# One written order for the mixing stage of block 1, in place of evenly spaced merging

## The chip, the cores and the metric

The kernel runs on one core of one Trainium2 chip. The metric is the device time of one execution in microseconds (us), the median of several. The core has five engines with queues of their own that run in order and meet only at semaphores: TensorE (PE, matrix products), VectorE (DVE), ScalarE (ACT), GpSimd (POOL) and SyncE (SP, which here issues the weight loads).

## The reference

The program is two layers of a first block (block 1: mixing, then an MLP) followed by two layers of another block (block 2), on 512 tokens of width 1024. The change concerns the mixing of block 1, which runs twice:

```python
h = rms_norm(x, g_mix_pre)
u = h @ w_in                       # 1024 -> 3200
aq, ak, av, cu, rq, rk, rv, rg = jnp.split(u, SPLITS, axis=-1)
y_att = chunk_attention(aq, ak, av, rel_bias)      # 6 heads, softmax with a bias table
y_conv = conv_module(cu, conv_w, conv_b, ...)      # gate, 31 depthwise taps, layer norm, silu
y_ret = retention(rq, rk, rv, rg)                  # 6 heads, rotary, decay mask, layer norm, gate
mix = jnp.concatenate([y_att, y_conv, y_ret], axis=-1) @ w_out
x = x + rms_norm(mix, g_mix_post)
```

## The kernel before

**Tiles.** Activations lie transposed, features on the 128 partitions and all 512 tokens along the row. The projection `w_in` is cut into units of 128 output features. For each unit ACT copies the raw weights to a rounded high part (L945), DVE takes the low part (L1406), and PE makes 24 matmuls (8 tiles of 128 inputs, three products each, L2027 to L2029, called one projection below). A unit's split runs two units ahead: it is issued by ACT and DVE at the place of an earlier projection in the order of steps.

**Names in the order.** `q`, `k`, `v` with a number 0 to 2 are the attention projections of a pair of heads, `cg` and `ca` those of the convolution, `rq`, `rk`, `rv`, `rg` those of retention; a name with `f` at its end is the projection, and the same name without it the transposition by PE that follows (L2242). `sq`, `sk` are the rotary swaps: one matmul (L2247), then three DVE operations (L1625, L1626, L1628). `rs0` to `rs23` are retention scores of one head and one block of 128 keys, with n = 512, 384, 256 or 128 columns (L2280; head h and block j are number 4h + j); DVE multiplies each by the decay mask while it empties the bank (L1715). `r_pv` is the product with the values (L2306), `r_out` ACT's copy of it. `lm`, `cm` are means (L2291, L2284) and `lv`, `cv` variances (L2294, L2288) of the layer norms. `taps` k is tap k of the convolution, two DVE operations (L1608), 62 in all.

**Banks.** Projections, transpositions, swaps, scores `rs`, means and variances take two PSUM banks (0 and 1) in turn, in the order in which they stand. PE may write the next of them only when the one before last has been emptied, by ACT for some and by DVE for others.

**Attention.** There are twelve attention steps (three pairs of heads, four blocks of queries). A step j goes through: scores on PE (L2107, L2109); bias and maximum on DVE (L1540, L1542); exponentials on ACT (L1029); reciprocal on DVE (L1528); scaling on POOL (L883); transpositions on PE (L2118); a copy on DVE for even steps (L1521) or ACT for odd (L1035); the product with the values on PE (L2129); after each fourth step ACT's copy of the result (L1039).

**What sets the order.** A list of steps is made once, and each engine walks it and issues its own part of each step. Before, an entry `att` k carries for PE the scores of step k, the transpositions of step k-2 and the value product of step k-3; for ACT the exponentials of k-1, the copy of k-2 and the output of k-3; for DVE the copy of k-2. An entry `weigh` k carries for DVE the reciprocal of k-1 and the bias and maximum of k. These entries, the projections, the retention heads and the taps are merged by `weave` (L234), which places each list at even distances within each of six stretches (L310 to L321):

```python
steps += weave(in_order(ret_qkv(1), "rv1"), heads(0), attend(8, 11), taps(16, 23))
```

Of the kernel before, what the change touches and what calls it, by code (L numbers as in the profile page):

```python
# [19 lines left out]
ALU = mybir.AluOpType  # L20
# [3 lines left out]
P = 128  # L24
D = 1024
S = 512
# [10 lines left out]
HD = 64  # L37
# [48 lines left out]
ACT_STEPS, DVE_STEPS = (2, 18), (79, 37)  # L86
NSA_PAIRS, T_LAG, O_LAG, P_BUFS = 3, 4, 5, 4
# [153 lines left out]

def plan_block1():
# [57 lines left out]
    def attend(a, z):  # L300
        return [(what, k) for k in range(a, z) for what in ("att", "weigh") if what == "att" or k <= n_att]

    def taps(a, z):
        return [("taps", k, k + 1) for k in range(a, z)]

# [3 lines left out]
    steps = qkv(0)  # L309
    steps.append(query(1))  # L310
    steps += [add(f"cg{t}", "fm", 1408 + 128 * t, frees="act", dst=A_SG + S * t, func="Sigmoid", keep=t == 0) for t in range(2)]
    steps.append(("g", "v0"))
    steps += [add(f"ca{t}", "fm", 1152 + 128 * t, frees="dve", glu=t) for t in range(2)]
# [6 lines left out]
    steps += weave([("mix", 0), gate(0), ("mix", 1), ("g", "lm0"), ("g", "cm"), gate(1), ("mix", 2), ("g", "lv0"), ("c_square",), gate(2), ("g", "cv"), ("g", "lm1"), ("early", 0), ("g", "lv1")], heads(2))  # L320
    steps += [("ahead",), ("early", 1), ("g", "lm2"), ("gated",), ("r_square", 2), ("rmul", 0), ("rmul", 1), ("early", 2)]  # L321
    steps += [("conv_out",), ("mix", 3), ("mix", 4), ("ln_set",), ("g", "lv2"), ("mix", 5), ("mix", 6), ("rmul", 2), ("mix", 7)]
# [145 lines left out]
def build(nc, x_in, cst, msk, tab1, tab2, scratch, out, w):  # L468
    with ExitStack() as ctx:
# [465 lines left out]
        def _(act):  # L935
# [85 lines left out]
            def attend(c, l, j):  # L1021

                e = j - EXP_LAG
                if 0 <= e < n1:
                    st, n = stat[:, e % 4, :], att_e[e]["n"]
                    act.wait_ge(c.maxed.sem, c.maxed.at(l, e + 1))
                    for head in HEADS:
                        p_ = att_p(e, head, n)
                        act.activation(p_, p_, ACT.Exp, bias=st[:, head:head + 1], accum_out=st[:, 2 + head:3 + head]).then_inc(c.exped.sem, 1)  # L1029
                k = j - TURN_LAG  # L1030
                if 0 <= k < n1 and k % 2:
                    act.wait_ge(c.turned.sem, c.turned.at(l, k + 1))
                    if k >= 2:
                        act.wait_ge(c.pv.sem, c.pv.at(l, k - 1))
                    act.activation(att_pt(k), bank[:, 4:6, 0:att_e[k]["n"]], ACT.Copy).then_inc(c.pt[1].sem, 1)  # L1035
                k = j - PV_LAG
                if 0 <= k < n1 and att_e[k]["i"] == QT - 1:
                    act.wait_ge(c.pv.sem, c.pv.at(l, k + 1))
                    act.activation(g(MIX + S * att_e[k]["p"]), bank[:, 6, :], ACT.Copy).then_inc(c.o_done.sem, 1)  # L1039
# [150 lines left out]
            for l in range(LAYERS):  # L1190
# [7 lines left out]
                for s in b["steps"][4:]:  # L1198
                    if s[0] == "g":
                        group(c, b, l, b["groups"][s[1]])  # L1200
                    elif s[0] == "att":
                        attend(c, l, s[1])
# [198 lines left out]
        def _(dve):  # L1401
# [112 lines left out]
            def attend(c, l, j):  # L1514

                k = j - TURN_LAG
                if 0 <= k < n1 and k % 2 == 0:
                    dve.wait_ge(c.turned.sem, c.turned.at(l, k + 1))
                    if k >= 2:
                        dve.wait_ge(c.pv.sem, c.pv.at(l, k - 1))  # L1520
                    dve.tensor_copy(att_pt(k), bank[:, 4:6, 0:att_e[k]["n"]]).then_inc(c.pt[0].sem, 1)  # L1521

            def weigh(c, l, j):

                k = j - EXP_LAG
                if k >= 0:
                    dve.wait_ge(c.exped.sem, c.exped.at(l, 2 * k + 2))
                    dve.reciprocal(stat[:, k % 4, 4:6], stat[:, k % 4, 2:4]).then_inc(c.rcp.sem, 1)  # L1528
                if j < n1:
                    e, n, st = att_e[j], att_e[j]["n"], stat[:, j % 4, :]  # L1530
                    dve.wait_ge(c.qk.sem, c.qk.at(l, j + 1))
                    if e["i"] == 0:
                        dve.wait_ge(c.h_in[e["p"] % 2].sem, c.h_in[e["p"] % 2].at(l, e["p"] // 2 + 1))
                    if j >= 2:
                        dve.wait_ge(c.turned.sem, c.turned.at(l, j - 1))
                    if j >= 4:
                        dve.wait_ge(c.scaled.sem, c.scaled.at(l, 2 * j - 6))
                    p_ = pair_tile(A_P[j % 2], n)
                    table = g(A_H[e["p"] % 2], 2 * S).rearrange("p (e n) -> p e n", e=2)[:, :, n - 1::-1]
                    dve.tensor_tensor(p_, bank[:, 2:4, 0:n], table, ALU.add).then_inc(c.biased.sem, 1)  # L1540
                    dve.wait_ge(c.biased.sem, c.biased.at(l, j + 1))
                    dve.tensor_reduce(st[:, 0:2], p_, AXX, ALU.max, negate=True).then_inc(c.maxed.sem, 1)  # L1542
# [277 lines left out]
            for l in range(LAYERS):  # L1820
# [7 lines left out]
                for s in b["steps"][4:]:  # L1828
                    if s[0] == "g":
                        group(c, b, l, b["groups"][s[1]])  # L1830
                    elif s[0] == "att":
                        attend(c, l, s[1])
                    elif s[0] == "weigh":
                        weigh(c, l, s[1])
# [189 lines left out]
        def _(pe):  # L2024
# [71 lines left out]
            def attend(c, b, l, j):  # L2096

                if j < n1:
                    p, i, n = att_e[j]["p"], att_e[j]["i"], att_e[j]["n"]
                    q = P * i  # L2100
                    if i == 0:
                        need(c, b, l, f"q{p}", f"k{p}", f"v{p}")
                    if j:
                        pe.wait_ge(c.biased.sem, c.biased.at(l, j))
                    for head in HEADS:
                        r = half(head)
                        pe.matmul(bank[:, 2 + head, 0:n], g(A_Q + S * p + q, P, r), g(A_K + S * p, n, r), start=True, stop=False)  # L2107
                    for head in HEADS:
                        ins = pe.matmul(bank[:, 2 + head, q:q + P], identb, chunked, start=False, stop=True)  # L2109
                    ins.then_inc(c.qk.sem, 1)  # L2110
                k = j - TURN_LAG
                if 0 <= k < n1:
                    if k:
                        pe.wait_ge(c.pt[(k - 1) % 2].sem, c.pt[(k - 1) % 2].at(l, (k - 1) // 2 + 1))
# [6 lines left out]
                if 0 <= k < n1:  # L2121
                    p, i = att_e[k]["p"], att_e[k]["i"]
                    pe.wait_ge(c.pt[k % 2].sem, c.pt[k % 2].at(l, k // 2 + 1))
                    if i == 0 and p:
                        pe.wait_ge(c.o_done.sem, c.o_done.at(l, p))
# [518 lines left out]
```

## Time and profile before

| | us |
|---|---|
| median of 3 runs | 3427.54 |
| lowest and highest | 3426.94, 3428.37 |
| the profiled execution: its time | 3425.86 |
| the profiled execution: its span, first to last instruction | 3424.0 |
| of the span: PE busy | 3349.4 |
| DVE, ACT, POOL busy | 1670.1, 1223.3, 236.9 |

The mixing of block 1 lies at 54 to 255 us of the span in the first layer and some 640 us later again in the second. A row of the time line gives start, duration, engine, line, operation and tile; in brackets stands how long the engine was idle before it and who ended that. A PE row of one float32 matmul counts as x2. Matmuls overlap in part, so a duration is longer than the distance to the next start; distances between starts are what adds up to time.

### The profile page before, as it was taken

To read this page: it belongs to the slowest core of one execution; us is meant where nothing else is said; L and a number is where in the kernel's file an instruction comes from. 1 tells how busy PE (TensorE), PEld (TensorE's weight loads), DVE (VectorE), ACT (ScalarE), POOL (GpSimd) and SP (SyncE) were. 2 spreads that over 40 slices of the span, in tenths; PEclk is the share of its full clock that TensorE was granted. 3 is DMA by queue.
4 is the path that set the end of the run, shared out by engine and by line. 5 is a ranking of instruction groups with operands and counts; after the bars stand their busy time and mean duration, and the time that the engine had idled before them with its cause. 6 is when DMAs were issued, how large, how long until landed. Compare 5 with 4: busy or idle time off the path is not lost.

```text
span 3424.0 us, 42157 instructions
## 1 busy us (share of the span) xinstructions
PE 3349.4 (98%) x15716; PEld 2623.2 (77%) x15716; DVE 1670.1 (49%) x2158; ACT 1223.3 (36%) x1831; POOL 236.9 (7%) x268
## 2 busy tenths in 40 slices
PE   8999999999999999999999999999999999999999
PEld 6657888776688887888766688888888876678887
DVE  6755443566544335443646554435443554654444
ACT  4343122432522233232454433334223454542333
POOL 1200000011010000000102300002000101300000
PEclk9999999999999999999999999999999999999999
DMA  6213322321243232332321133333333321023332
GB/s 170 64 47 87 96 95 98 92 81 50 68 101 97 98 104 74 96 95 97 87 60 29 31 104 93 97 98 94 98 98 98 93 72 34 19 88 98 93 97 74
DMA packets 434263, 288.19 MB, mean 84 GB/s; under 512 B 44529, under 2 KB 412317, under 8 KB 433897
## 3 DMA queue, kind: packets, MB, share of 16 engines
q1 hardware_dynamic: 431272, 280.02, 28.2%
q0 software_dynamic: 2736, 4.58, 0.9%
q10 hardware_dynamic: 144, 2.10, 0.2%
q8 instruction: 72, 1.18, 0.1%
q14 instruction: 39, 0.31, 0.0%
HBM read 284.53 MB, written 2.13 MB: 84 GB/s over the span
## 4 chain that ended last, share of the span: by engine, by line
PE 93%; DVE 3%; ACT 2%; issue 1%; DMA 0%; SPq 0%; DVEq 0%; ACTq 0%
PE bank L2027 27%; PE bank L2028 27%; PE bank L2029 27%; PE bank L2157 1%; PE bank L2203 1%; PE bank L2063 1%; PE bank L2179 1%; PE bank L2280 1%; PE bank L2247 1%; PE bank L2107 1%; ACT whi L945 1%; PE bank L2564 0%; DVE G L1562 0%; PE bank L2051 0%; PE bank L2129 0%
## 5 line engine op out<-in xcount | busy, mean ns | idle before, releaser
L2027 PE MATMUL bank<-hh,whi 128*128 128x512 f32 x2768 | 1093.1, 395 | 9.5 <-DVE G L1715 3.5
L2029 PE MATMUL bank<-hh,wlo 128*128 128x512 f32 x2768 | 1079.8, 390 | 0.0
L2028 PE MATMUL bank<-hl,whi 128*128 128x512 f32 x2768 | 1079.8, 390 | 0.0
L1406 DVE TENSOR_TENSOR wlo<-raw,whi 128x1024 fp32r<-128x1024 f32 (+2 forms) x534 | 647.0, 1213 | 318.1 <-ACT whi L945 303.7
L945 ACT ACTIVATE whi<-raw 128x1024 fp32r<-128x1024 f32 (+2 forms) x534 | 546.4, 1034 | 265.7 <-PE bank L2029 264.9
L2027 PEld LDWEIGHTS bank<-hh,whi 128*128 128x128 f32 x2768 | 521.3, 188 | 141.7 <-issue 33.1
L2029 PEld LDWEIGHTS bank<-hh,wlo 128*128 128x128 f32 x2768 | 521.0, 188 | 109.7
L2028 PEld LDWEIGHTS bank<-hl,whi 128*128 128x128 f32 x2768 | 521.4, 188 | 108.1 <-issue 2.6
L2027 PE MATMUL bank<-fshi,whi 128*128 128x512 f32 (+1 forms) x1358 | 525.9, 387 | 3.0 <-ACT G L1090 1.6
L2028 PE MATMUL bank<-fslo,whi 128*128 128x512 f32 (+1 forms) x1358 | 522.0, 384 | 0.0
L2029 PE MATMUL bank<-fshi,wlo 128*128 128x512 f32 (+1 forms) x1358 | 521.9, 384 | 0.0
L1755 DVE TENSOR_TENSOR fslo<-G,fshi 128x512 fp32r<-128x512 f32 x152 | 104.7, 692 | 460.8 <-ACT fshi L1130 460.8
L2027 PEld LDWEIGHTS bank<-fshi,whi 128*128 128x128 f32 x1358 | 255.6, 188 | 60.6 <-issue 5.6
L2029 PEld LDWEIGHTS bank<-fshi,wlo 128*128 128x128 f32 x1358 | 256.1, 189 | 51.0
L2028 PEld LDWEIGHTS bank<-fslo,whi 128*128 128x128 f32 x1358 | 255.9, 188 | 50.5 <-issue 1.0
L1130 ACT ACTIVATE fshi<-G 128x512 fp32r (+1 forms) x152 | 95.3, 631 | 539.8 <-PE bank L2029 539.8
L1286 ACT ACTIVATE G<-G 128x512 f32<-128x512 f32 x88 | 55.6, 632 | 619.2 <-DVE G L1907 619.1
L1907 DVE TENSOR_TENSOR G<-bank,G 128x512 f32<-128x512 f32 x88 | 60.9, 692 | 243.9 <-PE bank L2029 229.9
L1090 ACT ACTIVATE G<-bank 128x512 f32<-128x512 f32 x66 | 39.4, 597 | 279.7 <-PE bank L2029 279.7
L1910 DVE TENSOR_TENSOR G<-bank,G 128x512 f32 (+1 forms) x88 | 60.9, 692 | 147.4 <-PE bank L2029 147.4
L850 POOL TENSOR_TENSOR G<-G 128x512 f32<-128x512 f32 x21 | 33.3, 1585 | 1423.0 <-ACT G L971 1420.1
L1870 DVE TENSOR_TENSOR G<-bank,G 128x512 f32<-128x512 f32 x64 | 44.3, 692 | 167.0 <-PE bank L2029 158.9
(257 smaller groups left out, 2562.8 us busy)
## 6 DMA issues: line engine op xcount, KB each, us to landing
raw<-in_ffn_w_gate SPq DMA_DIRECT2D x88, 512.0 KB, 3.8
raw<-in_ffn_w_up SPq DMA_DIRECT2D x88, 512.0 KB, 3.8
raw<-in_ffn_w_down SPq DMA_DIRECT2D x88, 512.0 KB, 3.5
raw<-in_w_in SPq DMA_DIRECT2D x78, 512.0 KB, 4.0
raw<-in_w_up SPq DMA_DIRECT2D x64, 512.0 KB, 4.0
raw<-in_w_down SPq DMA_DIRECT2D x64, 512.0 KB, 3.4
raw<-in_w_out SPq DMA_DIRECT2D x16, 512.0 KB, 3.9
raw<-in_w_in SPq DMA_DIRECT2D x18, 256.0 KB, 3.5
```

What stands on the lines that cost most here:

```text
L945: act.activation(slot3(whi, s, m), slot3(raw, s, m), ACT.Copy).then_inc(c.hi_done.sem, 1)
L1090: act.activation(g(gr["dst"], S, r), bk[r[0]:r[1], :], act_func(gr.get("func")), scale=gr.get("scale", 1.0)).then_inc(evac, 1)
L1130: act.activation(fshi[:, 2 if paired else t % 2, :], f_tile(t + more), ACT.Copy).then_inc(c.f_hi.sem, 1)
L1286: act.activation(rt[t], tmp[t], ACT.Silu).then_inc(c.silu.sem, 1)
L1406: dve.tensor_tensor(slot3(wlo, s, m), slot3(raw, s, m), slot3(whi, s, m).bitcast(F32), ALU.subtract).then_inc(c.lo_done.sem, 1)
L1755: dve.tensor_tensor(fslo[:, fs, :], f_tile(t + more), fshi[:, fs, :].bitcast(F32), ALU.subtract).then_inc(c.f_lo.sem, 1)
L1870: dve.tensor_tensor(tmp[j % 2], bank[:, OUT_BANK + 1 + j, :], rstd, ALU.mult).then_inc(c.up_norm.sem, 1)
L1907: dve.tensor_tensor(tmp[t], bank[:, 4 + j, :], rstd, ALU.mult).then_inc(c.g_norm.sem, 1)
L1910: dve.tensor_tensor(f, bank[:, 4 + j, :], rstd, ALU.mult).then_inc(c.u_norm.sem, 1)
L2027: pe.matmul(o, wh, ah, start=start, stop=False)
L2028: pe.matmul(o, wh, al, start=False, stop=False)
L2029: return pe.matmul(o, wl, ah, start=False, stop=stop)
```

## The change

The attention entries are taken apart. There are now entries for PE alone (`a_scores`, `a_turns`, `a_values`), for ACT alone (`a_exps`, `a_move_act`, `a_out`) and for DVE alone (`a_bias`, `a_rcp`, `a_move_dve`), each in the same order within its engine as before. The six stretches are gone: one string of 216 letters says from which of six lists the next step is taken (f: projections and what follows them, p, a, d: attention on PE, ACT, DVE, h: retention heads, t: taps). Every instruction is issued as often as before, with the same operands and the same semaphores to wait on; the lags between the parts of an attention step are free. The change acts in both layers of block 1. The first six projections, the end of the stage (from `lv1` on) and block 2 keep their order.

```diff
+MIXING1_ORDER = (
+    "dffpftftdpatdtftadapdfpdfadpttpfdfpddtptpafdfppttttfadadpddafptdtpptffpapafpapddhfttadhppfpddhhhahtdhpftpafhpdahthppfdtp"
+    "hhfhadtdfpaatphdpdhfphdahphdhffttahhthfphtphftttffhhhphahffffhhhfhfffhhhhfhhhffffffffffffffffffff")
...
+def merged(order, **lists):
+
+    queues = {letter: iter(steps) for letter, steps in lists.items()}
+    return [next(queues[letter]) for letter in order]
...
-    steps += weave(in_order(qkv(1), "v1"), attend(0, 3), taps(0, 5))
-    r0 = ret_qkv(0)
-    steps += weave(in_order(r0, "rv0"), attend(3, 6), taps(5, 11))
-    steps += weave(in_order(qkv(2), "v2"), attend(6, 8), taps(11, 16))
-    steps += weave(in_order(ret_qkv(1), "rv1"), heads(0), attend(8, 11), taps(16, 23))
-    steps += weave(in_order(ret_qkv(2), "rv2"), heads(1), attend(11, n_att + PV_LAG), taps(23, TAPS))
...
+    for j in range(n_att + PV_LAG):
+        by_pe += staged(j, "a_scores") + staged(j - TURN_LAG, "a_turns") + staged(j - PV_LAG, "a_values")
+        by_act += staged(j - EXP_LAG, "a_exps") + staged(j - TURN_LAG, "a_move_act", odd) + staged(j - PV_LAG, "a_out", last)
+        by_dve += staged(j - TURN_LAG, "a_move_dve", even) + staged(j - EXP_LAG, "a_rcp") + staged(j, "a_bias")
...
+    steps = first_six + merged(MIXING1_ORDER, f=prepared, p=by_pe, a=by_act, d=by_dve, h=heads(0) + heads(1) + heads(2), t=[("taps", k, k + 1) for k in range(TAPS)])
```

The three pieces below show how it moves instructions. Line numbers are those of each version; the changed one is some 15 lines longer, so that L1406 of before is L1423 of the change, L2280 is L2298 and so on.

**First piece, DVE, from the gate of the convolution on.** TENSOR_TENSOR `wlo` is the low part of a weight unit, L1729 empties a `ca` bank, COPY from `bank` empties `k1`, and a TENSOR_TENSOR of `bank,G` with 128x2x128 columns and the TENSOR_REDUCE behind it are the bias and maximum of attention step 0. Before:

```order
L1728 MEMSET G 128x30
L1729 TENSOR_TENSOR G<-bank,G 128x512
L1406 TENSOR_TENSOR wlo<-raw,whi 128x1024
L1728 MEMSET G 128x30
L1729 TENSOR_TENSOR G<-bank,G 128x512
L1605 TENSOR_SCALAR G<-G,prm 128x512 x2
L1406 TENSOR_TENSOR wlo<-raw,whi 128x1024
L1738 COPY G<-bank 128x512
L1540 TENSOR_TENSOR G<-bank,G 128x2x128
L1542 TENSOR_REDUCE stat<-G 128x2
```

And now:

```order
L1555 TENSOR_TENSOR G<-bank,G 128x2x128
L1557 TENSOR_REDUCE stat<-G 128x2
L1423 TENSOR_TENSOR wlo<-raw,whi 128x1024
L1743 MEMSET G 128x30
L1744 TENSOR_TENSOR G<-bank,G 128x512
L1423 TENSOR_TENSOR wlo<-raw,whi 128x1024
L1743 MEMSET G 128x30
L1744 TENSOR_TENSOR G<-bank,G 128x512
L1620 TENSOR_SCALAR G<-G,prm 128x512 x2
L1423 TENSOR_TENSOR wlo<-raw,whi 128x1024
```

The bias of step 0 stood behind both gates, two weight parts, tap 0 and the copy of `k1`; it now stands ahead of all of them.

**Second piece, PE, at the projection `rk1`.** L2107 and L2109 are attention scores of step 8, L2118 transpositions of step 6, L2129 the value product of step 5, L2280 (L2298) the retention scores. Before:

```order
L2029 MATMUL bank<-hh,wlo 128x512
L2107 MATMUL bank<-G 128x128 x2
L2109 MATMUL bank<-m_sb 128x128 x2
L2118 MATMUL bank<-c_sb,G 128x128 x6
L2129 MATMUL bank<-G 64x128 x4
L2280 MATMUL bank<-G 128x512
L2280 MATMUL bank<-G 128x384
L2027 MATMUL bank<-hh,whi 128x512
```

And now:

```order
L2046 MATMUL bank<-hh,wlo 128x512
L2298 MATMUL bank<-G 128x512
L2123 MATMUL bank<-G 128x128 x2
L2125 MATMUL bank<-m_sb 128x128 x2
L2135 MATMUL bank<-c_sb,G 128x128 x6
L2044 MATMUL bank<-hh,whi 128x512
```

`rs4` (512 columns) stood directly ahead of `rs1` and `rk1`; it now stands ahead of the attention work, and `rs1` (384) has gone behind `rk1`, next to `rs5`.

**Third piece, ACT, around the projection `q2`.** L1090 (L1103) empties a projection's bank, L1094 (L1107) that of a transposition, L1029 (L1040) are exponentials, L945 (L958) the high part of a weight unit, L1035 (L1047) the copy of step 3. Before:

```order
L1029 ACTIVATE G,stat<-G,stat 128x128 x2
L1035 ACTIVATE G<-bank 128x1024
L1094 ACTIVATE G<-bank 128x4x128
L945 ACTIVATE whi<-raw 128x1024
L1090 ACTIVATE G<-bank 128x512
L1029 ACTIVATE G,stat<-G,stat 128x256 x2
```

And now:

```order
L1107 ACTIVATE G<-bank 128x4x128
L1040 ACTIVATE G,stat<-G,stat 128x128 x2
L1047 ACTIVATE G<-bank 128x1024
L1040 ACTIVATE G,stat<-G,stat 128x256 x2
L958 ACTIVATE whi<-raw 128x1024
L1103 ACTIVATE G<-bank 128x512
```

The exponentials of step 5 (256 columns) stood behind the weight part and the emptying of `q2`; they now stand ahead of both.

## Rows read from the trace of the kernel before

**Rows 1.** The page, part 1: busy time of each engine

```profile
PE 3349.4 (98%) x15716; PEld 2623.2 (77%) x15716; DVE 1670.1 (49%) x2158; ACT 1223.3 (36%) x1831; POOL 236.9 (7%) x268
```

**Rows 2.** Windows: stretch, length, busy us (instructions) by engine, granted clock, DMA share, GB/s

```profile
54.05:233.90 179.85, 174.47 (x860) 118.27 (x860) 118.54 (x182) 59.35 (x112) 27.74 (x26) 1.00 0.22 62
```

**Rows 3.** Waits of PE, 50 to 260 us: us in total, times, longest

```profile
PE bank L2027 <- DVE G L1715: 1.8, 2, 0.9
...
PE bank L2280 <- ACT G L1090: 0.5, 2, 0.3
```

**Rows 4.** The same in the second layer, 640 to 860 us

```profile
PE bank L2107 <- DVE G L1540: 1.1, 1, 1.1
```

**Rows 5.** Time line of PE, 65 to 81 us

```profile
72.49 0.70 PE L2107 MATMUL bank<-G 64*128 64x256 f32 x4 [1.11 <-DVE G L1540]
```

**Rows 6.** Time line of PE, 127 to 139 us

```profile
136.50 1.12 PE L2280 MATMUL bank<-G 64*128 64x512 f32 x4
138.50 0.47 PE L2027 MATMUL bank<-hh,whi 128*128 128x512 f32 x1 [0.88 <-DVE G L1715]
```

**Rows 7.** Time line of PE, 156 to 164 us

```profile
156.69 0.48 PE L2280 MATMUL bank<-G 64*128 64x128 f32 x2
...
157.87 1.13 PE L2247 MATMUL bank<-G,c_sb 128*128 128x512 f32 x2
158.92 0.92 PE L2107 MATMUL bank<-G 64*128 64x384 f32 x4
159.77 0.28 PE L2109 MATMUL bank<-m_sb 128*128 128x128 bf16 x2
...
160.21 1.09 PE L2129 MATMUL bank<-G 128*64 128x128 f32 x16
161.14 0.82 PE L2306 MATMUL bank<-G 128*64 128x256 f32 x8
161.89 0.66 PE L2242 MATMUL bank<-c_sb,G 128*128 128x128 f32 x4
163.28 1.09 PE L2280 MATMUL bank<-G 64*128 64x512 f32 x2 [0.73 <-issue]
```

**Rows 8.** Time line of PE, 182 to 187 us

```profile
183.88 0.70 PE L2280 MATMUL bank<-G 64*128 64x256 f32 x2
184.81 0.70 PE L2280 MATMUL bank<-G 64*128 64x256 f32 x2 [0.24 <-DVE G L1628]
185.44 0.87 PE L2306 MATMUL bank<-G 128*64 128x384 f32 x4
```

**Rows 9.** Time line of PE, 204.5 to 208 us

```profile
204.80 1.67 PE L2280 MATMUL bank<-G 64*128 64x512 f32 x4
206.71 1.12 PE L2291 MATMUL bank<-G,c_sb 128*128 128x512 f32 x2 [0.24 <-DVE G L1715]
```

**Rows 10.** Time line of PE, 217 to 222 us

```profile
217.24 1.45 PE L2280 MATMUL bank<-G 64*128 64x256 f32 x4
219.13 1.10 PE L2294 MATMUL bank<-G,c_sb 128*128 128x512 f32 x2 [0.43 <-ACT G L1070]
```

**Rows 11.** Groups of DVE by form, 54.05 to 233.9 us: busy us, mean ns | idle before

```profile
L1406 DVE TENSOR_TENSOR wlo<-raw,whi 128x1024 fp32r<-128x1024 f32 x20 | 24.4, 1220 | 12.3 <-ACT whi L945 12.3
```

**Rows 12.** Time line of POOL, with and without taps beside it

```profile
100.33 3.43 POOL L883 TENSOR_SCALAR G<-G,stat 128x512 f32<-128x512 f32 x2 [6.96 <-DVE stat L1528]
...
141.45 3.11 POOL L883 TENSOR_SCALAR G<-G,stat 128x512 f32<-128x512 f32 x2 [11.57 <-DVE stat L1528]
```

**Rows 13.** Time line of DVE, at 101 us

```profile
100.92 1.40 DVE L1608 SCALAR_TENSOR_TENSOR G<-G,prm 128x512 f32<-128x512 f32 x2
```

**Rows 14.** The chain that ended last, 181 to 186 us: start, us, what

```profile
184.07 0.70 DVE G L1628
```

**Rows 15.** Windows as in rows 2, after the stage's end, in both layers

```profile
240.00:250.00 10.00, 7.57 (x24) 5.24 (x23) 5.41 (x9) 8.38 (x12) 0.00 (x0) 0.83 0.37 101
...
880.00:890.00 10.00, 7.57 (x31) 5.38 (x30) 5.47 (x9) 7.97 (x12) 0.00 (x0) 1.00 0.32 90
```

More of the change, by code:

```diff
@@ L320, in plan_block1, with staged @@
-    steps += weave([("mix", 0), gate(0), ("mix", 1), ("g", "lm0"), ("g", "cm"), gate(1), ("mix", 2), ("g", "lv0"), ("c_square",), gate(2), ("g", "cv"), ("g", "lm1"), ("early", 0), ("g", "lv1")], heads(2))
-    steps += [("ahead",), ("early", 1), ("g", "lm2"), ("gated",), ("r_square", 2), ("rmul", 0), ("rmul", 1), ("early", 2)]
-    steps += [("conv_out",), ("mix", 3), ("mix", 4), ("ln_set",), ("g", "lv2"), ("mix", 5), ("mix", 6), ("rmul", 2), ("mix", 7)]
+    def staged(k, what, wanted=range(n_att)):
+        return [(what, k)] if 0 <= k < n_att and k in wanted else []
@@ new lines, in plan_block1 @@
+    first_six = qkv(0)
+    first_six.append(query(1))
+    first_six += [add(f"cg{t}", "fm", 1408 + 128 * t, frees="act", dst=A_SG + S * t, func="Sigmoid", keep=t == 0) for t in range(2)]
+    prepared = [("g", "v0")]
+    prepared += [add(f"ca{t}", "fm", 1152 + 128 * t, frees="dve", glu=t) for t in range(2)]
+    prepared += in_order(qkv(1), "v1")
+    prepared += in_order(ret_qkv(0), "rv0")
+    prepared += in_order(qkv(2), "v2")
+    prepared += in_order(ret_qkv(1), "rv1")
+    prepared += in_order(ret_qkv(2), "rv2")
@@ new lines, in plan_block1 @@
+    prepared += [("mix", 0), gate(0), ("mix", 1), ("g", "lm0"), ("g", "cm"), gate(1), ("mix", 2), ("g", "lv0"), ("c_square",), gate(2), ("g", "cv"), ("g", "lm1"), ("early", 0), ("g", "lv1")]
+    prepared += [("ahead",), ("early", 1), ("g", "lm2"), ("gated",), ("r_square", 2), ("rmul", 0), ("rmul", 1), ("early", 2)]
+    prepared += [("conv_out",), ("mix", 3), ("mix", 4), ("ln_set",), ("g", "lv2"), ("mix", 5), ("mix", 6), ("rmul", 2), ("mix", 7)]
+    steps = first_six + merged(MIXING1_ORDER, f=prepared, p=by_pe, a=by_act, d=by_dve, h=heads(0) + heads(1) + heads(2), t=[("taps", k, k + 1) for k in range(TAPS)])
@@ new lines, in att_turns @@
+            def att_turns(c, l, k):
+                if k:
+                    pe.wait_ge(c.pt[(k - 1) % 2].sem, c.pt[(k - 1) % 2].at(l, (k - 1) // 2 + 1))
+                pe.wait_ge(c.scaled.sem, c.scaled.at(l, 2 * k + 2))
+                for head in HEADS:
+                    for kt in range(att_e[k]["i"] + 1):
+                        ins = pe.transpose(bank[:, 4 + head, P * kt:P * kt + P], att_p(k, head, att_e[k]["n"])[:, P * kt:P * kt + P], ident)
+                ins.then_inc(c.turned.sem, 1)
@@ L2105, in attend, with att_values @@
+            def att_values(c, l, k):
+                p, i = att_e[k]["p"], att_e[k]["i"]
+                pe.wait_ge(c.pt[k % 2].sem, c.pt[k % 2].at(l, k // 2 + 1))
+                if i == 0 and p:
+                    pe.wait_ge(c.o_done.sem, c.o_done.at(l, p))
+                for kt in range(i + 1):
                     for head in HEADS:
                         r = half(head)
-                        pe.matmul(bank[:, 2 + head, 0:n], g(A_Q + S * p + q, P, r), g(A_K + S * p, n, r), start=True, stop=False)
@@ L2120, in attend @@
-                k = j - PV_LAG
[L2121 to L2125, printed above, removed]
-                    for kt in range(i + 1):
-                        for head in HEADS:
-                            r = half(head)
-                            ins = pe.matmul(bank[r[0]:r[1], 6, P * i:P * i + P], g(A_V + 384 * kt + HD * (2 * p + head), HD),
-                                            att_pt(k)[:, head, P * kt:P * kt + P], start=kt == 0, stop=kt == i)
-                    ins.then_inc(c.pv.sem, 1)
+                        ins = pe.matmul(bank[r[0]:r[1], 6, P * i:P * i + P], g(A_V + 384 * kt + HD * (2 * p + head), HD),
+                                        att_pt(k)[:, head, P * kt:P * kt + P], start=kt == 0, stop=kt == i)
```

152 lines of the change are left out of this document (71 added, 81 removed).

## The prediction

> **What bounds the kernel now.** I read the busy times first: PE is busy for 98% of the span, DVE for half and POOL hardly at all [rows 1]. So time goes down only where PE stands still, or where its own work gets shorter, and the change issues the same matmuls. The windows then say how much stands still in the stretch that is re-ordered: from 54.05 to 233.90 us PE is busy 174.47 of 179.85 us [rows 2], 5.4 us idle. A wait costs more than its idle time, because matmuls that follow each other overlap and the first ones behind a wait don't; I therefore take distances between starts. The waits by releaser show what PE waited for there: DVE's emptying of a score bank (L1715), ACT's emptying of a projection (L1090) and others [rows 3]. The second layer shows the same pattern; its wait for the bias at L1540 is 1.1 us [rows 4], that of the first 1.11 [rows 5]. I count one layer and double it. DVE has 118.54 and ACT 59.35 us of work in 179.85 us [rows 2]: neither is short of time on the whole, the waits come from where a step stands in a queue, and that is what the change touches.
>
> **The waits that the new order takes away,** each as the distance to PE's next start less the time of the work itself.
> (a) Scores of step 1 wait 1.11 us [rows 5] for the bias of step 0, which stood on DVE behind the copy of `k1`. Now it stands ahead, and two projections (`ca1`, `k1`) lie on PE between the scores of step 0 and of step 1. Gain 1.1.
> (b) `rs4` with `rs1`, then `rk1`, takes 138.50 - 136.50 = 2.0 us, where the two scores pass in 1.1 [rows 6]; `rk1` waits for DVE to empty the bank of `rs4`. The row [rows 3] counts two such waits, the other before `rk2` (behind `rs12`, `rs9`). Now scores and transpositions lie between `rs4` and `rk1`, and for `rk2` the transpositions stand behind it and the value product and `rs12` ahead, so that its bank, that of `rs8`, is emptied during `rs12`. Gain 2 x 0.9 = 1.8.
> (c) `rs3` and `rs7` take 157.87 - 156.69 = 1.18 us for some 0.45 us of work, since the second bank is still that of a projection that ACT empties [rows 7]; `rs11` and `rs15` likewise, the second of two such waits [rows 3]. Now `rpv1` and the value product of step 6 stand between `rv1f` and `rs3`, and `sk2` with the transpositions of step 11 between `rs11` and `rs15`. Gain 2 x 0.73 = 1.5.
> (d) `rv1`, then `rs8`: 163.28 - 161.89 = 1.39 us for 0.6 [rows 7]: `rs8` needs ACT's copy of the transposition just made. Now `rq2` and a whole attention step stand between. Gain 0.8.
> (e) `rs10` and `rs14`: 185.44 - 183.88 = 1.56 us [rows 8], where one pass takes 0.63; `rs14` waits for DVE to finish the swap `sq2`. Now `rv2f`, 5.5 us, stands between. Gain 0.9.
> (f) `rs20` with `rs17`, then `lm0`: 206.71 - 204.80 = 1.91 us [rows 9] for 1.1. Gain 0.8.
> (g) `rs18` with `rs22`, then `lv0`: 219.13 - 217.24 = 1.89 us [rows 10] for 0.63; they waited for ACT to empty `rg1`, and `lv0` for a square that stood behind that too. Now `rs21` and `rpv8` stand between `rg1` and `rs18`. Gain 1.3.
> Sum 8.2 us.
>
> **What it gives back.** Two scores of a pair of heads that stand next to each other pass in the time of one: `rs4` with `rs1`, four instructions, shows 1.12 us [rows 6], `rs8` alone, two instructions, 1.09 [rows 7]. So what counts is the number of passes. Before there are 6 of 512 columns, 3 of 384, 3 of 256 and 4 of 128 (counting a pair by its longer half, and pairs parted by a wait alone as one, since I took their whole wait as gain). Now there are 5, 4, 5 and 4. With 1.1 us for 512 [rows 6], 0.85 for 384 (the distance at the attention scores of that width, 159.77 - 158.92, [rows 7]) and 0.63 for 256 [rows 8] that is -1.1 + 0.85 + 1.26 = 1.0 us more. And one new wait is sure: `rs16`, `rs20`, `rs17` now stand in one row, and the third needs the bank of the first emptied by DVE, the situation of (b): 0.9 us. The wait before `cv` stays, behind other scores. Together 1.9.
>
> **What moves and is hidden.** DVE gets the bias of step 0 ahead of a weight part and a `ca` bank. Behind it wait PE's `k1` (the weight part) and `ca1`'s successor in the bank. The scores of step 0 come behind one projection, at some 60 us; bias and maximum of 256 columns take under 1 us by their width against the 1024 columns of a weight part, which takes 1.2 us [rows 11]: ready at some 62 us, needed at 65.8, a projection later. ACT gets the exponentials of step 2 ahead of the copy of `v1`, and those of step 5 ahead of a weight part and of `q2`'s bank; the second is the longest wait that the change adds, and I work it out below as the rival that ends on the other side. The last operations (from `lv1` on) hang on PE's `lm1`, `lv1` and on the ACT and DVE work behind them, in unchanged order, so they move as a whole. SP's weight loads follow DVE's low parts, which are at most 6 us later in place and are used two units later; PE never waits for one of them in this stretch.
>
> **The sum.** 8.2 - 1.9 = 6.3 us per layer, 12.6 for both. On the profiled execution's own 3425.86 us that makes 3413.3. The median of the three runs is 1.7 us above that execution, so on the median's scale the forecast is 3427.54 - 12.6 = 3414.9 us.
>
> **A rule of the notes against the trace.** POOL's scaling of a step of 512 columns takes 3.11 us alone and 3.43 with two taps beside it [rows 12]; the two taps, 1.40 us for both [rows 13], began while POOL was at work and took no longer than elsewhere. So here the two engines hardly disturb each other: 0.3 us, on POOL. The Trainium skill, page "SBUF — State Buffer", section "Who interferes with whom", states that a VectorE instruction with two SBUF inputs and a GpSimd instruction that reads SBUF exclude each other, the later one waiting for the whole of the earlier. By that rule the taps would have waited; the trace does not bear it out at this place.
> As a mechanism of this kernel the question matters, and it is the first rival. Before, DVE's reciprocal is followed by the next step's bias, which reads PSUM, so POOL's scaling runs beside that. Now in 5 of 12 steps taps or a weight part follow the reciprocal (steps 0, 2, 3, 5, 9).
>
> **The rivals.**
> *DVE and POOL take turns.* If each tap waited for POOL's scaling, DVE would be 3.1 us later behind step 3 [rows 12]. The bias of step 4 is by my count ready 1.4 us before PE needs it, so PE would lose 1.7 us per layer: 3414.9 + 3.4 = 3418.3. For it only the 0.3 us of rows 12; against it the taps of rows 13. 10%.
> *The tight places give way.* Behind `sk1` PE has a value product and two retention products, 161.89 - 160.21 = 1.7 us [rows 7], and the transposition of `rv1`, 0.6, before `rq2` needs the bank; DVE needs three operations of 0.7 us for the swap [rows 14], 2.0 us since they overlap a little. That leaves 0.3 us. Behind `sk0` it is some 0.7 us before `q2`, at the transpositions of step 4 (behind four taps, reciprocal and POOL) 1.6. If all three come 1.3 us later than my count, PE loses 1.0 + 0.6 + some of the third and its restarts, about 2.5 us per layer: 3420. For it: my counts come from one walk along the queues, to 0.3 us at best. 14%, half of it within the bound of no change.
> *More is won.* `rs17`'s wait may be hidden, or the swaps' order save restarts: up to 1.5 us per layer, 3411.9. 12%.
> *The clock.* Behind the stage's end, PE's granted clock was 0.83 of full over 10 us in the first layer and 1.00 in the second, at the same work [rows 15]: a short spell at the lower of the two levels (1.2 GHz), worth 0.17 x 10 = 1.7 us, came after thinly filled PE time in one and not in the other. With all later work moved by 6 and 13 us such spells can fall otherwise, by one or two in either direction: 3411.5 to 3418.3. 8%.
> *ACT stands still and takes PE with it.* The exponentials of step 5 wait for its maximum, which on DVE stands behind four taps, and behind them on ACT wait the high part for `v2f` and `q2`'s bank, which `v2f` takes over. From the swap `sk0`'s end DVE needs 8 x 0.7 for the taps [rows 13], then 1.4 for bias and maximum (twice the 0.7 of an operation of that width, [rows 14]); ACT some 2.4 for exponentials, weight part and copy (an estimate: it is no slower than DVE at like widths), DVE 1.2 for the low part [rows 11]: 10.6 us, against `q2`, `k2` and an attention step on PE, 14 us. Margin 3.5 to 4 us. It costs time only beyond that, and makes the kernel slower only if DVE is more than 3.7 + 6.3 = 10 us late there, in each layer. At 13 us late it would be 3414.9 + 2 x 9.3 = 3433.5. Nothing in rows 13 shows taps of nearly three times their length. 3%.
>
> **How the numbers follow.** The forecast has 53%, with its own range 3412 to 3417.5. The range 3410 to 3421 takes in the larger gain, the turns of DVE and POOL, the clock and most of the tight places, and leaves out some 12%. A difference of 0.2% (6.9 us) is about what a measurement can tell from no change. Faster by more: 53 + 10 + 12 + 8 + half of 14, less some for what I have not seen, 0.85. Within: 0.11. Slower: 0.04.
>
> **What would show it.** In the changed kernel's time line PE's idle time from the first `ca` projection to `lv1` should fall from 5.4 us to near 2; the wait for L1540 should be gone, that for L1715 stand once, before `rs17`; `lv1` should begin some 6 us earlier in the first layer and 12 in the second; the waits behind it should be as before. The forecast is wrong if PE waits for L1628 before `q2` or `rq2`, for ACT before `v2f`, or for POOL before transpositions, and if taps beside L883 are longer than 0.75 us each.

## The result and the profile after

The changed kernel takes 3407.15 us (median of 5 runs, 3406.06 to 3410.7); the kernel before took 3427.54 us (median of its 5 runs beside it). The ratio is 0.9942, 95% interval 0.9928 to 0.9957: faster by 20.4 us. The prediction was 3414.9 us with a range of 3410 to 3421: the sign was right, the gain was larger than the range allowed. The changed kernel was run once more later (`after_again`): 3409.01 against 3426.01 us, ratio 0.9951 (0.9937 to 0.9964). The two measurements give 20.4 and 17.0 us.

The changed kernel's page, part 1 (engine, busy us, share, instructions), against [rows 1]:

```profile
PE 3337.7 (98%) x15712; PEld 2623.6 (77%) x15716; DVE 1672.0 (49%) x2158; ACT 1222.6 (36%) x1831; POOL 248.9 (7%) x268
```

PE is busy 11.7 us less with the same matmuls (four records are missing). So not only waits went: busy steps also follow each other at shorter distances. POOL is busy 12 us longer. The window of the re-ordered stretch, from the first `ca` projection to `lv1`, columns as in [rows 2]:

```profile
56.11:226.38 170.27, 168.92 (x859) 118.24 (x860) 119.79 (x182) 59.11 (x112) 33.00 (x26) 1.00 0.24 66
```

It is 170.27 us long where it was 179.85 [rows 2]: 9.6 us less per layer. PE's idle time fell from 5.4 to 1.35 us, which is 4.0 of it; the other 5.5 us are shorter distances between busy matmuls. The waits of PE between 50 and 250 us (engine, line, waited for: us in all, times, longest) that lie in this window, against [rows 3]:

```profile
PE bank L2298 <- DVE G L1730: 0.8, 1, 0.8
...
PE bank L2306 <- DVE G L1730: 0.4, 1, 0.4
```

The wait for the bias is gone, and the wait for DVE's emptying of a score bank stands twice, before `rs17` and before `cv`. The sum had both; the prediction's list of signs counted only the first. Where [rows 5] shows a wait of 1.11 us, the changed kernel's time line shows none:

```profile
73.37 0.70 PE L2123 MATMUL bank<-G 64*128 64x256 f32 x4
```

Below, a step's *distance* is the time from PE's start of it to PE's start of the next step, the measure that the prediction used. Between two executions of one kernel it repeats to 0.04 us or better, while their whole times scatter by several us. *The stretch* is the time from `v0` to `lv1`, 181.18 us before and 171.60 after.

**Where the 18.7 us between the two profiled executions are.** For an execution I add up: the start of `v0`, twice the stretch, and half of the time during which the trace shows the granted clock at the lower level (1.2 GHz), since work there takes twice as long. Here, with no time at the lower clock inside the stretch, what is left of the span is the same in both:

| | start of v0 | stretch | lower clock | rest of the span |
|---|---|---|---|---|
| before | 52.72 | 181.18 | 39.3 | 2989.3 |
| after | 54.79 | 171.60 | 36.0 | 2989.3 |

So -18.7 = +2.1 (a later start of the stretch in this execution, not an effect of the order, which is the same up to there) - 2 x 9.58 - 1.6 (clock). The rest agrees better than the account deserves: over the other runs without a lowered clock in the stretch it lies between 2987.7 and 2990.0 us. The clock's 1.6 us is one spell, at 244 us of the span, that of [rows 15]; it is gone, and the others lie at the same work as before. Nothing else behind `lv1` took part.

### The profile page after: what moved, and what is told of

Same layout as the page of the kernel before. It is cut to its first block, busy times and chain, and to the rows that moved or that the text cites. A ratio compares the mean times of both kernels' runs of the same rounds, so it can differ in the third digit from the quotient of the medians.

```text
span 3405.3 us, 42157 instructions
## 1 busy us (share of the span) xinstructions
PE 3337.7 (98%) x15712; PEld 2623.6 (77%) x15716; DVE 1672.0 (49%) x2158; ACT 1222.6 (36%) x1831; POOL 248.9 (7%) x268
## 3 DMA queue, kind: packets, MB, share of 16 engines
q8 instruction: 72, 1.18, 0.1%
## 4 chain that ended last, share of the span: by engine, by line
PE 93%; DVE 3%; ACT 2%; issue 1%; DMA 0%; SPq 0%; DVEq 0%; ACTq 0%
PE bank L2044 27%; PE bank L2046 27%; PE bank L2045 27%; PE bank L2175 1%; PE bank L2221 1%; PE bank L2080 1%; PE bank L2197 1%; PE bank L2298 1%; ACT whi L958 1%; PE bank L2265 1%; PE bank L2586 0%; PE bank L2123 0%; DVE G L1577 0%; PE bank L2147 0%; PE bank L2068 0%
## 5 line engine op out<-in xcount | busy, mean ns | idle before, releaser
L1423 DVE TENSOR_TENSOR wlo<-raw,whi 128x1024 fp32r<-128x1024 f32 (+2 forms) x534 | 646.9, 1213 | 309.8 <-ACT whi L958 295.5
L958 ACT ACTIVATE whi<-raw 128x1024 fp32r<-128x1024 f32 (+2 forms) x534 | 546.4, 1034 | 272.9 <-PE bank L2046 272.4
L1103 ACT ACTIVATE G<-bank 128x512 f32<-128x512 f32 x66 | 39.3, 596 | 249.5 <-PE bank L2046 249.4
```

Of the source, the lines that this page charges most:

```text
L958: act.activation(slot3(whi, s, m), slot3(raw, s, m), ACT.Copy).then_inc(c.hi_done.sem, 1)
L1103: act.activation(g(gr["dst"], S, r), bk[r[0]:r[1], :], act_func(gr.get("func")), scale=gr.get("scale", 1.0)).then_inc(evac, 1)
L1423: dve.tensor_tensor(slot3(wlo, s, m), slot3(raw, s, m), slot3(whi, s, m).bitcast(F32), ALU.subtract).then_inc(c.lo_done.sem, 1)
```

## Experiments

The experiments that start from the kernel before are written in the new form, with steps in one order; the diffs show the order, one step a line where it matters. S, T and V with a number are attention scores, transpositions and value product of that step; R is DVE's reciprocal, B its bias, t a tap.

### Does PE's order alone bring it, or that of ACT and DVE?

`pe_new`: PE's steps in the new order, ACT's and DVE's attention steps and the taps at their old places. `pe_old`: the reverse.

> PE's steps in the changed kernel's order; the attention steps and taps of ACT and DVE stay where they were before, each behind the same projection. Theory 1 (the gain is PE's order: fewer waits there and cheaper neighbours): only the wait for the bias of step 0 comes back, 1.3 us per layer, so the gain is 20.4 - 2.6 = 17.8 us: 3409.7 us. Rival (ACT's and DVE's places carry the gain): under half of it, 3417 us or more, with PE waits for biases or copies.

> The other half: PE's steps in the old order, the attention steps and taps of ACT and DVE at the changed kernel's places. Theory 1: only the wait for the bias of step 0 goes, 1.3 us per layer: 3427.5 - 2.6 = 3424.9 us. Rival (ACT's and DVE's places carry the gain): 3417 us or less.

Measured: 3444.72 us, ratio 1.0046 (1.003 to 1.0063), and 3445.6 us, ratio 1.0048 (1.0031 to 1.0065). Theory 1 fell in both, and so did the rival, which needed `pe_old` at 3417 us or less: either half alone is 18 us *slower* than the kernel before, with a stretch of 188.6 and 190.9 us. In `pe_new`, ACT's time line shows where the longest wait comes from:

```profile
124.64 0.60 ACT L1052 ACTIVATE G<-bank 128x512 f32<-128x512 f32 x1 [12.48 <-PE bank L2147]
125.14 1.99 ACT L958 ACTIVATE whi<-raw 128x1024 fp32r<-128x1024 f32 x2
```

and PE's, behind it:

```profile
129.03 1.22 PE L2123 MATMUL bank<-G 64*128 64x512 f32 x2 [4.43 <-DVE G L1555]
```

V3 has moved behind `v2f` on PE, but ACT's copy of its result (L1052) stands at its old place, ahead of two weight parts. ACT stands for 12.48 us, DVE's low parts and bias follow late, and the scores of step 7 wait 4.43 us. In `pe_old` the mirror image: DVE takes up the bias of step 0 ahead of the banks of `ca0` and `ca1`, while PE makes these scores only behind `ca1`. DVE waits 11.21 us, and `k1` 2.8 us for its bank:

```profile
67.19 0.43 DVE L1555 TENSOR_TENSOR G<-bank,G 128x256 f32<-128x256 f32 x1 [11.21 <-PE bank L2125]
```

The waits are not the whole loss. Behind the wait of 4.43 us PE's granted clock (the last number but two) was at its lower level:

```profile
129.00:132.40 3.40, 3.38 (x12) 1.88 (x13) 3.40 (x5) 1.31 (x4) 1.04 (x2) 0.50 0.47 138
```

The scores of step 7 take 2.20 us there, to the next step's start, for 1.18 in the changed kernel. In the two stretches of `pe_new` 30.7 us ran at the lower clock, in those of `pe_old` 17.1, in those of the kernel before and of the changed one none. Half of that, 15 and 9 us, is my estimate of the clock's part; against the kernel before the two stretches are 16.0 and 17.8 us longer in sum.

What follows: the gain belongs to no engine's order. A step that moves on one engine takes its releaser's and its reader's places with it.

### Do shorter distances come from the neighbour?

Of 9.58 us, 2.4 lie in steps that no term of my sum touched; the largest part is 1.2 us of attention transpositions. In the changed kernel five of them are no longer followed by a value product. Two runs put this neighbour back and take it away.

`glued`, from the changed kernel (and likewise V1, V2, V3, V5 behind T2, T3, T4, T6):

```diff
 T1
+V0
 rk0
 ...
 sq0
-V0
```

> The changed kernel with the value products 0, 1, 2, 3 and 5 put back directly behind the transpositions of steps 1, 2, 3, 4 and 6. Theory 1 (a step's time depends on the shape of its neighbour: a full-array transposition before a 64-column product costs 0.17 to 0.20 us more than before a projection): the distances of these transpositions go back from 0.36, 0.58, 0.79, 0.15, 0.58 to 0.54, 0.76, 0.99, 0.32, 0.76 us, 0.88 per layer in sum, 3407.2 + 1.8 = 3409.0 us. Rival (these were small waits that the changed ACT and DVE places removed): the distances stay, 3407.2 us.

`apart`, from the kernel before, the reverse:

> The kernel before, with these five value products parted from the transpositions as in the changed kernel, and nothing else moved (but for ACT's copy of step 3's values, which follows its product). Theory 1: the five distances fall as above, 0.88 us per layer: 3427.5 - 1.8 = 3425.7 us. Rival: the distances stay, and nothing is gained, 3427.5 us.

Measured: 3411.61 us, ratio 0.9961 (0.9946 to 0.9975), and 3426.2 us, ratio 0.9993 (0.9983 to 1.0002). Neither total can tell 1.8 us from the clock's scatter; the distances decide. In us, with the step that follows:

| | T1 | T2 | T3 | T4 | T6 |
|---|---|---|---|---|---|
| before (V follows) | 0.54 | 0.76 | 0.99 | 0.32 | 0.76 |
| after (a projection follows) | 0.36 | 0.58 | 0.79 | 0.15 | 0.58 |
| glued (V follows) | 0.54 | 0.76 | 0.97 | 0.32 | 0.76 |
| apart | 0.36 | 0.58 | 0.90 (rv0) | 0.15 | 0.76 (rs4) |
| values_full (full-array V follows) | 0.45 | 0.66 | 0.88 | 0.22 | 0.66 |

The distances follow the neighbour each way, 0.88 us per layer in `glued` and 0.62 in `apart`. Where another step than a projection came behind the transpositions in `apart`, which my expectation overlooked, the gain is less: half before `rv0` (transpositions), nothing before `rs4` (a score). The stretch is 0.79 us shorter in `apart`, and 1.50 us longer in `glued`: there `rk1` also stands directly ahead of `rs1` and `rs5`, which take 0.76 and 0.84 us for 0.43 and 0.58. The trace names no wait there; that `rs5` can't pass beside `rs1` because ACT has not yet emptied `rk1`'s bank fits it, but is not tested. PE's time line at T1, before and after:

```profile
87.28 0.61 PE L2118 MATMUL bank<-c_sb,G 128*128 128x128 f32 x4
87.81 0.44 PE L2129 MATMUL bank<-G 128*64 128x128 f32 x4
```

```profile
88.14 0.61 PE L2135 MATMUL bank<-c_sb,G 128*128 128x128 f32 x4
88.50 0.47 PE L2044 MATMUL bank<-hh,whi 128*128 128x512 f32 x1
```

The busy time of the transpositions is 0.61 in both; only the start of what follows tells the difference. `glued` and `apart` don't say why a value product starts later. It uses half of the array (`128*64`). `values_full` keeps the old order and gives it all of it:

```diff
-pe.matmul(bank[r[0]:r[1], 6, P * i:P * i + P], g(A_V + 384 * kt + HD * (2 * p + head), HD), ... start=kt == 0, stop=kt == i)
+pe.matmul(bank[:, 6, P * i:P * i + P], g(A_V + 384 * kt + HD * 2 * p, 2 * HD), ... start=kt + head == 0, stop=kt == i and head == 1)
```

> The kernel before, where a value product takes 128 columns of weights (both heads' values) in place of 64 for each head: all of TensorE's array in place of a half, so the shape is that of the transposition ahead of it. The two heads' results are summed into each other, so this part of the output is another. Theory 1 (what costs 0.17 to 0.20 us is the change of shape): the transpositions of steps 1 to 4 and 6 take 0.36, 0.58, 0.79, 0.15, 0.58 us though a value product still stands behind them, and so do those of the other steps; the products themselves take nearly twice as long, since two heads no longer pass side by side (0.12 us for each 128 columns by the 0.48 of a 512-column pass of the means: 14.4 against 8.4 us per layer). Time 3427.5 + 2 x (6.0 - 1.9) = 3435.7 us. Rival (the product's own wait or its start costs it): the distances stay at 0.54, 0.76, 0.99, 0.32, 0.76, and 3439.5 us.

Measured, one run: 3429.17 us. All eleven transpositions ahead of a value product are shorter, but by 0.09 us and not by 0.18:

```profile
88.40 0.61 PE L2135 MATMUL bank<-c_sb,G 128*128 128x128 f32 x4
88.85 0.61 PE L2146 MATMUL bank<-G 128*128 128x128 f32 x4
```

The stretch grew by 3.99 us (the products took 5.6 us more, near the 6.0 of my estimate); that the time grew by only some 3 us is the clock, 29.8 us at the lower level in this execution. So each theory has half of it. With the same table read for every transposition in all traces: before a half-array step (V, a score) they take the full distance, before a full-array step in plain fp32 (a transposition, a swap as at T8 and `sk1`, 0.23 against 0.32, the wide V) 0.09 less, before a projection, whose operands are fp32r, 0.12 to 0.20 less. The first 0.09 goes with the change of shape. The Trainium skill, page "TensorEngine Tiling (Array Packing)", section "Key Properties", says that changing the tiling mode drains TensorE; the traces agree, and 0.09 us is what it cost behind a short matmul here. Between two half-array shapes it is as much: `rs6` takes 0.31 us before a retention product and 0.22 before an attention score of its own shape, V9 0.59 before a score and 0.49 before a retention product. Not every change shows it: behind the swap `sk1` a value product started after 0.95 us, behind `sk2` a transposition after 0.96. The other 0.09 us goes with the kind of the next step's operands; what in it costs them I did not test.

### One wait by itself

`bias_first`, from the kernel before:

```diff
 S0
+B0
 t0
 k1
-B0
```

> The kernel before with one step moved: on DVE the bias of step 0 stands ahead of a tap and of the copy of projection k1. Theory 1: the wait before the scores of step 1 goes, k1's distance falls from 6.83 to 5.53 us in each layer, and nothing behind gives it back: 3427.5 - 2.6 = 3424.9 us. Rival (a gain this early is taken back by a later wait): less than 1 us in all, 3426.5 to 3427.5 us.

Measured: the distance of `k1` 5.65 us (was 6.83), every other step the same to 0.05, the stretch 179.90 us, 1.28 less. The scores of step 1 start 18.58 us behind `v0`, as in the changed kernel; there `k1` itself takes 5.53, but `ca0` and `ca1` 0.12 more. Nothing behind took it back: theory 1, in the trace. The total, 3425.02 us, ratio 0.9997 (0.9987 to 1.0006), can't tell 2.6 us from none.

### POOL and DVE

`quiet`, from the changed kernel; t2 likewise ahead of R0, and t7, t8 ahead of R3:

```diff
+t5
+t6
 R2
 S3
-t5
-t6
```

> The changed kernel with taps 2, 5, 6, 7 and 8 ahead of the reciprocals of steps 0, 2 and 3 in place of behind them, so that POOL's scaling runs beside no tap there. If DVE's taps and POOL's scaling take turns: the scaling of step 2 falls from 4.96 to 2.5 us and that of step 3 from 3.75 to 3.1, and no row of DVE's taps is over 2.8 us for four; PE waits for neither, so the time stays within 0.5 us of 3407.2. If the long scalings come from another cause they stay. If these turns cost PE something the trace hides, the kernel is over 1 us faster, 3406 us or less.

In the changed kernel, POOL's scaling of a step (L896) and the four tap operations (two taps) beside it:

```profile
88.43 4.96 POOL L896 TENSOR_SCALAR G<-G,stat 128x384 f32<-128x384 f32 x2 [4.12 <-DVE stat L1541]
98.16 3.75 POOL L896 TENSOR_SCALAR G<-G,stat 128x512 f32<-128x512 f32 x2 [4.77 <-DVE stat L1541]
...
127.49 2.46 POOL L896 TENSOR_SCALAR G<-G,stat 128x384 f32<-128x384 f32 x2 [11.11 <-DVE stat L1541]
```

```profile
88.26 2.97 DVE L1623 SCALAR_TENSOR_TENSOR G<-G,prm 128x512 f32<-128x512 f32 x4
...
97.98 3.59 DVE L1623 SCALAR_TENSOR_TENSOR G<-G,prm 128x512 f32<-128x512 f32 x4
```

In `quiet` the first of these scalings, and what DVE had there (the second takes 4.00 us):

```profile
91.01 3.36 POOL L896 TENSOR_SCALAR G<-G,stat 128x384 f32<-128x384 f32 x2 [6.78 <-DVE stat L1541]
```

```profile
88.10 2.74 DVE L1623 SCALAR_TENSOR_TENSOR G<-G,prm 128x512 f32<-128x512 f32 x4
...
90.83 1.21 DVE L1423 TENSOR_TENSOR wlo<-raw,whi 128x1024 fp32r<-128x1024 f32 x1
91.95 1.22 DVE L1555 TENSOR_TENSOR G<-bank,G 128x1024 f32<-128x1024 f32 x1
```

A scaling of 384 columns takes 2.46 us undisturbed and 4.96 beside four tap operations, which take 2.97 in place of 2.74, and a weight's low part (L1423), which follows them at 91.14. Without taps it takes 3.36: the low part alone, which has two inputs in SBUF like a tap operation, costs POOL 0.9. The bias (L1555), whose one input is in PSUM, costs nothing. At step 3 the two engines share the loss: 3.75 us for 3.10 on POOL, 3.59 for 2.73 on DVE. So they do disturb each other, and the expected 2.5 and 3.1 us failed because the low part stood beside the scaling. It is not a full turn each: at step 2 both were done 5.13 us after the first tap's start, and one after the other they would have taken 6.4 (my estimate, 2.46 + 2.74 + 1.21). The rule that I weighed in the prediction (the Trainium skill, page "SBUF — State Buffer", section "Who interferes with whom") is borne out as to which instructions disturb each other, and I had set it aside wrongly; that one waits for the whole of the other these rows don't show. In the kernel before, a tap operation (100.92 to 101.67) lies whole within POOL's first instruction (100.33 to 101.89, 1.57 us), and neither is longer than elsewhere. The waits of PE show none for POOL in either kernel, and the stretch is 171.73 us in `quiet`: the transpositions of step 3 start 0.14 us later there, just behind the later scaling, and no more is lost. That it ran at 3414.1 us, ratio 0.9959 (0.9943 to 0.9974), 7 us above the changed kernel, is no effect of these taps: its profiled execution spent 49.7 us at the lower clock, the changed kernel's 36.0.

### Is the clock the kernel's doing?

`quiet` and the changed kernel once more, side by side on one chip:

> The kernel of the run quiet once more: taps ahead of three reciprocals, PE's stretch v0 to lv1 as long as the changed kernel's (171.7 against 171.6 us), but 13.7 us more at the lower clock, 6.8 us of time. Theory 1 (where the spells at the lower clock fall belongs to the kernel): again some 50 us at the lower clock and 3414 us. Rival (chance of the run or of the chip): as the changed kernel beside it, within 2 us.

> The changed kernel itself, on the chip on which the next two run, so that they are compared with it there. By the account of the profiles so far (time = start of v0 + twice the stretch from v0 to lv1 + half the time at the lower clock + 2990.0 us), it takes 3405.5 to 3407.5 us. If quiet's 7 us come from that chip and not from the kernel, it is near 3412 instead.

Measured: 3409.98 us (ratio 0.9953, 0.9937 to 0.9968) and 3409.01 us. The rival holds: 42.5 us at the lower clock in both profiled executions, at the same places to 1 us. `paired2` (below), run with them on the same chip, has 42.6 us at these places to 2 us. So it is not the kernel; whether it is the chip or chance stays open. Over 14 profiles it was 30 to 74 us, and 30 to 62 without the two kernels that have long waits. Windows of the changed kernel and of its second run (columns as above; the granted clock is the last but two):

```profile
1710.00:1725.00 15.00, 15.00 (x77) 11.67 (x77) 8.38 (x11) 7.77 (x11) 0.00 (x0) 0.89 0.38 74
```

```profile
1710.00:1725.00 15.00, 15.00 (x67) 11.93 (x67) 7.92 (x12) 7.08 (x11) 0.00 (x0) 0.66 0.37 71
```

PE is busy for all of it in both and gets 77 matmuls done in one and 67 in the other. The same program differs from run to run by this, and a difference of 2 us between two kernels shows only in their distances.

### Can the tail be made shorter still?

`paired`: the order from `rg0` on, and `rs8`, `rs12` side by side ahead of T9.

```diff
 rg0 rpv7
-V11 rs16 rs20 rs17 lm0 cm rg1 rs21 rpv8 rs18 lv0 rg2 rs22 rpv9 rs19 rs23 cv rpv10
+rs16 rs20 V11 rs17 rs21 rpv8 lm0 cm rg1 rs18 lv0 rg2 rs22 rpv9 rs19 rs23 rpv10 cv
```

> The changed kernel with retention scores put side by side: rs8 with rs12 behind attention scores 11 and ahead of their transpositions; in the tail rs16, rs20, the value product 11, rs17, rs21, the product rpv8, then lm0; rpv10 ahead of cv. Theory 1 (two scores of a head pair share one pass when nothing lies between, and a wait costs what it shows): one pass of 512 columns less (0.9 us), the wait before rs17 (0.78) and a pass of 384 columns (0.7) less, the wait before cv (0.38) less, one more change of shape (0.2): 2.6 us per layer, 3407.2 - 5.2 = 3402.0 us. Rival (the banks that now turn round faster are not yet empty): PE waits for L1730 before rk2 or rs21 in place of it, 3405 us or more.

Measured: 3408.07 us, ratio 0.994 (0.9927 to 0.9954), the stretch 170.91 us: 0.68 shorter, not 2.6. `rs8` and `rs12` take 0.53 + 0.53 us where they took 1.05 + 1.05 apart; `rs20`, `rs17` and `rs21` together are shorter by 1.26, `cv` and its neighbours by 0.35. But `lv0` now waits 1.2 us, and `early0`, before `lv1`, takes 0.43 more. I tried `lm0` earlier:

```diff
-V11 rs17 rs21 rpv8 lm0 cm
+V11 rs17 lm0 rs21 rpv8 cm
```

> As paired, but lm0 stands between rs17 and rs21, so that the square for lv0 is ready as in the changed kernel. Theory 1: the wait of 1.2 us before lv0 goes; left are one pass less at rs8 and rs12 (0.96), rs20 without the wait before rs17 (0.46) and cv (0.35), less 0.1: v0 to lv1 takes 171.6 - 1.7 = 169.9 us, and 3407.2 - 3.4 = 3403.8 us if as long is spent at the lower clock, 1.7 us more or less for each spell of 3.4 us. Rival (another bank or square is late now): 170.9 us or more, as paired.

Measured: 3410.64 us, ratio 0.9962 (0.9949 to 0.9976), the stretch 171.95 us. `lv0` waits as before, although `lm0` comes 1.2 us earlier than in the changed kernel, counted from `v0`; my reason was wrong. ACT's time line shows the right one:

```profile
208.76 0.60 ACT L1103 ACTIVATE G<-bank 128x512 f32<-128x512 f32 x1 [9.08 <-PE bank L2046]
209.25 0.62 ACT L1253 ACTIVATE fshi<-G 128x512 fp32r<-128x512 f32 x1
209.77 0.62 ACT L1083 ACTIVATE G<-G 128x512 f32<-128x512 f32 x1
```

```profile
210.54 0.67 PE L2312 MATMUL bank<-G,c_sb 128*128 128x512 f32 x1 [1.19 <-ACT G L1083]
```

The square (L1083) stands behind the copy of `rg1` (L1103), and what covered these three operations were `rs21` and `rpv8` between `rg1` and `lv0`. `paired3` puts them back and keeps only `rs8`, `rs12` and V11 between `rs20` and `rs17`:

> Only the two changes of paired2 that lie behind no wait for ACT: rs8 with rs12 ahead of the transpositions 9, and the value product 11 between rs20 and rs17; from lm0 on, the order is the changed kernel's, with rs21 and rpv8 between rg1 and lv0 again. Theory 1 (in paired and paired2 lv0 waited for its square, which stands on ACT behind the copy of rg1, and rs21 and rpv8 had covered that; and cv's gain was given back before lv1): 0.87 + 0.46 - 0.1 = 1.2 us per layer, v0 to lv1 in 170.4 us, 3404.8 us with as long at the lower clock as the changed kernel. Rival (the chain over ACT and DVE sets the tail whatever stands on PE ahead of it): lv1 comes no earlier, 171.5 us, 3407 us.

Measured: the stretch 170.35 us, 1.25 less than the changed kernel's, as expected. The time is 3408.71 us (3404.34 to 3416.18), ratio 0.9939 (0.9927 to 0.9952), with 61.5 us at the lower clock in the profiled execution. By its distances it is the best kernel here; by its times it can't be told from the changed one.

## Why the prediction missed

**What held.** The waits and their places. (a) measured 1.30 us for 1.1, and 1.18 alone in `bias_first`; (d) 0.79 for 0.8; the new wait before `rs17` 0.78 for 0.9; the wait before `cv` stayed. The waits behind `lv1` are as before, and `lv1` came 7.5 us earlier in the first layer although this execution began 2.1 us later. No tight place gave way, ACT was never late.

**The priced terms held too.** (b), (c), (e), (f) and (g) with what the passes and the wait before `rs17` give back were to bring 4.4 us together. At the places that they name the distances fell by 4.1: 1.79 at the two of (b), forecast 1.8; 0.85 and 0.34 at those of (c), forecast 0.73 each; 0.31 at `rs10` and `rs14`, forecast 0.9 less a pass of 0.63; 0.22 from `rs16` to `rs17`, where 0.15 was left of (f); 0.64 at `rs18` and `rs22` for 0.63. In (c) `rs11` and `rs15` lost their common pass; my count set that off against `rs19` and `rs23`, which gained one. `paired` shows the size of this: two scores of 512 columns side by side take 1.06, apart 2.10.

**The step that failed.** "The change issues the same matmuls", and so I took a step's distance as its own and summed only waits and passes. It is that of a pair: it depends on the step behind. What the sum had no term for brought 3.3 us per layer, all that the forecast missed. Of it, 0.9 lies beside the scores: 0.35 at `lv0`, 0.30 at `rs19` and `rs23`, 0.28 at `rs2`, `rs6` and attention scores 9 and 10. The other 2.4 lie in steps that I had not looked at: the five transpositions brought 0.90, the others 0.32, swaps, means and value products the rest, of which the projections right behind a mean, a variance or a swap (`rg1`, `rg2`, `rv2f`, `early0`) took 1.3 back. A run of its own shows only the five transpositions; the rest is read from the distances, and some of it may have other causes. The rows to see it stood in the profile before, had I compared T-steps with different neighbours. By steps, per layer: 1.3 + 0.8 + 5.1 + 2.4 = 9.6 us, twice that 19.2 for a forecast 12.6. "More is won" had 1.5 us per layer for it, but from a hidden wait and the swaps; it was 3.3.

**The rule about SBUF.** I wrote that the trace does not bear it out, from one place with the two operations of one tap beside it [rows 12, 13]. The 0.3 us there were its trace. One of my signs of a wrong forecast did come: tap operations beside L896 took up to 1.18 us, over the 0.75 that I had set. The result did not suffer, since POOL's results are needed late, but that was luck of the argument: the rival's price, 1.7 us per layer, rested on a margin of 1.4 us at T4, which did hold.

**The clock** fell as the rival had it: 1.6 us between the two profiles (half of 39.3 - 36.0); between others it is up to 13 us (half of 61.5 - 36.0), more than I allowed. The miss does not hang on it: without those 1.6 us the two profiles are still 17.1 us apart.

## What to carry to other kernels

Sum a re-ordering by distances between starts for each pair of neighbours, not by waits alone: behind short matmuls, a neighbour of another array shape cost 0.09 us and one of another operand kind as much again, and from `v0` to `lv1` the array's shape changes 65 times in the changed kernel where it changed 86 times before. At 0.09 us each those 21 would be 1.9 of the 3.3 us (an estimate, and a high one, since not every change showed it). Move a step together with the steps on other engines that read it or release it, since each half of this change alone lost 18 us where the whole won 20, a good part of it by the clock behind the long waits. When one run's clock differs from the next, compare stretches, and keep what covers a chain over another engine (here `rs21` and `rpv8` before `lv0`) though it looks like filling.

## What the runs showed of the hardware

Three things I had not expected. POOL's scaling of 384 columns took 2.46 us alone, 3.36 beside a weight's low part (two SBUF inputs) and 4.96 beside four tap operations and a low part. The time at the lower clock differed between runs of the same program with PE busy in the windows shown: 36.0 and 42.5 us in two executions of the changed kernel, 3 us of time. And 128-column transpositions in the full array were followed 0.09 us sooner by a full-array step than by a half-array one, and another 0.09 us sooner by a projection.
